# Two generated filters in a two-block kernel: where the first transform weights are split, and where the second filter's modulations stand

## The reference

```python
mod = c_act @ mod_w[i] + mod_b[i]                       # 1024 x 6144, six vectors
u = causal_dwconv(u, dw_w) + dw_b                       # 31 taps, first block
# second block, filters of the Hyena branch
hdn = jnp.sin(freq * (hdn @ fw2 + fb2))
h = (hdn @ fw3 + fb3).reshape(L, HYENA_ORDER, 2, D_HYENA)
h = h * jnp.exp(-t * deltas)[:, None, None, :]
circ = jnp.concatenate([h_fwd, zeros, h_bwd[:0:-1]], axis=0)
return jnp.fft.rfft(circ, axis=0)                       # one for each of the two orders
```

## Time and profile before

| what | value |
|---|---|
| median of 3 runs | 3285.05 us (3284.10 to 3286.02) |
| profiled execution, its own time | 3293.38 us |
| its span | 3291.6 us |
| TensorE matmul busy | 3100.8 us, 94% |
| VectorE busy | 1710.9 us, 52% |
| ScalarE busy | 1012.1 us, 31% |
| GpSimd busy | 399.9 us, 12% |
| TensorE clock granted, mean | 0.962 |

### The profile page before, as it was taken

The page is one execution under the profiler, slowest core; times in us unless marked ns, Lnnn a source line. Parts: engine busy times, 40 slices in busy tenths (PEclk is TensorE's granted clock), DMA queues, the critical chain, the costliest instruction groups (busy, mean ns, idle before and its releaser), DMA issues. The chain is left out here.

```text
span 3291.6 us, 33493 instructions
## 1 busy us (share of the span) xinstructions
PE 3100.8 (94%) x13786; PEld 2500.3 (76%) x13786; DVE 1710.9 (52%) x1776; ACT 1012.1 (31%) x1203; POOL 399.9 (12%) x161
## 2 busy tenths in 40 slices
PE   7999869899999999899999999799999999999996
PEld 3784457778888888778888877677877788888885
DVE  5698886655655554574411176677455322223225
ACT  3455444332212222233221133476222311111111
POOL 0496540000000000000200144000110000000000
PEclk8998879899999999899999999899998999999998
DMA  5114423232222321322332343521331202112112
GB/s 207 58 33 160 161 82 115 76 104 71 96 83 97 122 86 63 108 77 77 124 113 103 117 151 124 133 62 50 128 114 58 76 26 64 48 39 61 39 45 109
DMA packets 96192, 301.24 MB, mean 92 GB/s; under 512 B 11205, under 2 KB 15045, under 8 KB 95847
## 3 DMA queue, kind: packets, MB, share of 16 engines
q1 hardware_dynamic: 96040, 299.09, 27.8%
HBM read 251.34 MB, written 47.71 MB: 91 GB/s over the span
## 5 line engine op out<-in xcount | busy, mean ns | idle before, releaser
L708 PE MATMUL ps<-mainr,wh 128*128 128x512 f32 (+1 forms) x6592 | 1781.8, 390 | 31.0 <-issue 12.7
L708 PEld LDWEIGHTS ps<-mainr,wh 128*128 128x128 f32 x6592 | 1238.4, 189 | 290.4 <-issue 34.5
L708 PE MATMUL ps<-mainr,wl 128*128 128x512 f32 (+1 forms) x3296 | 1029.8, 389 | 0.0
L708 PEld LDWEIGHTS ps<-mainr,wl 128*128 128x128 f32 x3296 | 622.6, 189 | 128.4
L1714 DVE TENSOR_TENSOR wl<-raw,wh 128x1024 fp32r<-128x1024 f32 (+2 forms) x272 | 294.6, 1085 | 459.4 <-ACT wh L1236 459.2
L1236 ACT CAST wh<-raw 128x1024 fp32r<-128x1024 f32 (+2 forms) x320 | 282.0, 885 | 750.3 <-PE ps L708 539.6
L1973 DVE TENSOR_TENSOR mainf<-mainf,ps 128x1024 f32<-128x1024 f32 x80 | 97.6, 1220 | 215.1 <-PE ps L708 215.1
L754 PE MATMUL ps<-mainr,wh 128*128 128x512 f32 x576 | 165.7, 412 | 36.4 <-issue 22.0
L2014 DVE SCALAR_TENSOR_TENSOR ps<-mainf,vec,ps 128x1024 f32<-128x1024 f32 (+1 forms) x174 | 181.0, 1103 | 2.5 <-ACT ps L1425 2.3
L2498 POOL TENSOR_TENSOR tmp<-tmp,mainf 128x1024 f32<-128x1024 f32 x8 | 27.5, 3439 | 1162.2 <-DMA mainf<-in_rope 1099.0
L2465 POOL TENSOR_TENSOR wl<-raw,wh 128x1024 fp32r<-128x1024 f32 x48 | 114.7, 2400 | 425.0 <-ACT wh L1236 425.0
(11 more groups left out here) (236 smaller groups left out, 2903.9 us busy)
## 6 DMA issues: line engine op xcount, KB each, us to landing
raw<-in_mod_w SPq DMA_DIRECT2D x48, 512.0 KB, 4.2
raw<-in_ada_w SPq DMA_DIRECT2D x48, 512.0 KB, 3.6
raw<-in_f_up SPq DMA_DIRECT2D x44, 512.0 KB, 4.0
raw<-in_g_up SPq DMA_DIRECT2D x44, 512.0 KB, 3.5
raw<-in_w_in SPq DMA_DIRECT2D x40, 512.0 KB, 4.1
raw<-in_pw SPq DMA_DIRECT2D x24, 512.0 KB, 3.8
sc_x<-mainf SPq DMA_DIRECT2D x24, 512.0 KB, 2.6
mainf<-sc_x SPq DMA_DIRECT2D x24, 512.0 KB, 6.7
```

The source lines that it names most:

```text
L708: ins = e.matmul(out, wt[:, a:b], xs[n], start=kk == 0 and t == 0, stop=kk == kt - 1 and t == 2)
```

## The change

Two things. First, the two functions `modulation_weights` on ScalarE and VectorE are taken out, with their calls. The first two weight tiles of each filter's transform are split at the end of step 7 of the filter instead, behind the lower halves of its taps and the convolution step after them on VectorE, and behind the upper halves on ScalarE. Second, in the second filter the modulations stand behind steps 0, 4 and 6, where they stood behind 0, 3 and 5. In the first they stay behind 0, 3 and 5. What is computed is the same, and so are the list of weights and the number of instructions.

```diff
     for s in range(32):
         out.append(("f", s))
-        if s % 16 in (0, 3, 5):
+        if s in (0, 3, 5, 16, 20, 22):
             out.append(next(mods))
...
-    def modulation_weights(kind, jb, ahead):
-        for kp in range(4):
-            split_to(k.W[kind, jb, kp] + ahead)
...   scalar_program, filter_step, behind the upper halves
                 e.copy(k.TAPS_OF(0, step)[:, n, :], k.BANK("taps", o, step, n)).then_inc(*k.to("thi", o, step, n))
+            if step == 7:
+                split_to(k.W["filt", o, 0, 0] + 2)
             return
...   scalar_program and vector_program, walk through OTHER
         else:
-            modulation_weights(kind, s, HL)
             row = (kind, s)
...   vector_program, filter_step, behind the lower halves
             conv_steps(turns, 1)
+            if step == 7:
+                split_to(k.W["filt", o, 0, 0] + 2)
             return
```

## The result

The changed kernel takes 3292.29 us in the median of 19 runs (3287.27 to 3296.84); the kernel before takes 3282.99 in 19 runs beside them (3280.68 to 3287.34). The ratio is 1.0027, with a 95% interval of 1.0021 to 1.0033: **9.3 us slower**, between 6.9 and 10.8 by the interval. Forecast were 3293.7 us and +8.6. Spans and times of single executions of one kernel differ by several us, so a stage is compared by its own rows.

A forecast was written before the change was run, and what follows sets the result against it. Tap steps are bound by a loop through three engines, product steps by TensorE (first filter) and VectorE (second). Terms 3.0 + 5.3 + 0.3 = +8.6 us on 3285.05 gave 3293.7 us, range 3288.5 to 3298.5.

The forecast's parts named there:

- The wait that goes: Behind the third modulation: lower halves of the taps come 3.61 us earlier in the first filter, 2.44 in the second.
- The late first product: First filter, step 8: TensorE waits for VectorE's lower halves, convolution and split, starting 3.94 us later than before.
- Its speed: Step 8's product in each filter, partly at half-speed clock after a standstill: 7.6 us taken, 5.39 at full clock.
- No cover: Behind the first products: TensorE full in the first filter, VectorE in the second, so the whole delay passes on.
- The middle modulation: Second filter: one more sparse step before it may start it at the lower clock; 0 to 0.66 us, +0.3 taken.
- Loads keep up: Second filter: raw tiles of the moved modulations are asked for one modulation ahead, so no term for loads.
- The sum: First filter +3.0, second filter +5.3, middle modulation +0.3: +8.6 us in all.
- The anchor: Median of the kernel before, taken as 3285.05 us, on which the forecast of 3293.7 us stands.
- GpSimd first: Rival: GpSimd takes the shared port before VectorE's split, +2.2 us in each filter, +13.0 in all; chance 0.15.
- The clock that stays up: Rival: both first products take 5.39 us, 2.2 less each, +4.2 in all, 3289.3 us; chance 0.12.
- The shift of the port's phase: Rival, second filter's tail: VectorE's splits and sums meet no GpSimd, saving 13.4 us, -4.8 in all; chance 0.08.
- The hidden start: Rival: waits gained count in full and the late first product is hidden by slack, -6.0 us, 3279.0; chance 0.05.

The follow-up runs named there:

- splits-alone kernel: Changed kernel with the second filter's modulations back behind steps 0, 3 and 5, so only the weight splits moved; 3293.15 us against 3284.49, ratio 1.0024.
- the kernel that kept TensorE busy: Changed kernel plus 28 and 22 extra, overwritten matmuls ahead of the first product in the two filters; 3289.19 us, ratio 1.0013 of before.

## Why the prediction was right, and where its sizes were off

- **The wait that goes.** Expected 3.61 us. In the changed kernel the lower halves of step 6 come 11.30 us behind the third modulation's start (279.95 to 291.25), where they came 14.91 behind it (280.36, to 295.27): 3.61. In the second filter 2.44 was expected. The splits-alone kernel, whose modulations stand as before, shows it in its second profile: step 7's lower halves came 16.07 us behind the third modulation's start (383.90 to 399.97), where before they came 18.52 behind it (380.01, to 398.53), 2.45 less. The size of this wait hangs on when the loads land: in the second profile of before the two casts waited 2.58 and 1.03 us for them, where they waited 2.35 and 0.28 in the first, and the lower halves came 20.03 us behind.
- **The late first product.** Expected 3.94 us later; 19.79 for 15.85 us is 3.94, and 19.79 for 15.81 in the second profiles is 3.98. The three parts (lower halves, convolution, split) stood as computed, and VectorE came first at the port by 0.21 us where 0.23 was computed.
- **Its speed.** I took 7.6 us for each of the two first products, between bounds of 7.05 and 8.15. Measured were 8.11 and 7.28 in the first profile, 7.51 and 7.18 in the second: the mean was about right, and that the clock is the cause is shown by the kernel that kept TensorE busy. The 5.39 us at full clock was 0.25 short: from a product's start to its copy a step takes 5.64, since a step's first matmul starts before the copy of the one before it.
- **No cover.** Steps 9 to 15 took 37.9 us in both profiles of both kernels, and the tail 66.3 to 66.8: TensorE in the first filter and VectorE in the second pass on everything. Right.
- **The filters one by one.** They were less exact than the sum. To the first filter's copy 3.0 us were forecast, and 3.5 measured in the first pair of profiles (27.90 and 24.40), 4.4 in the second (27.31 and 22.91): step 8 before took 8.55 us in the execution from which I computed, and 7.10 in the other. For the second filter 5.6 were forecast (5.3 and 0.3), and 6.3 and 4.9 measured.
- **The middle modulation.** Mis-sized in both pairs: +0.3 us taken, 0.66 the bound, +0.89 (9.99 for 9.10) and +0.64 (9.80 for 9.16) measured. The upper bound was the first filter's 9.76 us, and this one ran even a little slower. No term stood for the second filter's first modulation, with its wait for a load inside it: it took 11.27 and 9.84 us before and 11.69 and 11.42 in the changed kernel. "Loads keep up" holds for the moved modulations, not for this one, which waited 2.6 to 3.0 us for its last tile in both kernels.
- **The sum.** 8.6 us forecast; 10.0 in the first pair of profiles (197.9 and 187.9), 9.0 in the second (196.5 and 187.6), 9.3 in the times.
- **What stood on luck.** The parts of the sum that came out exactly are chains of waits. Where the clock falls differs between executions, and single terms were off by up to 1.6 us for that, in both directions. The anchor was not exact either: with more runs the kernel before is at 3282.99 us and not 3285.05, and the forecast time was 1.4 us too high for that although the step was 0.7 too small.
- **The rivals.** GpSimd first did not happen. Made to happen, it cost what the rows say for a lead of 0.72 us: 2.39 + 1.08 - 0.72 - 1.23 = 1.52 us, measured 1.48. The clock that stays up did not happen by itself; made to happen it gave 3.2 to 3.9 of the 4.4 us. The shift of the port's phase did not happen: in the tail the long weight splits took 3.17, 3.35 and 2.30 us (3.15, 3.36 and 2.30 before), and the four sums 3.2 to 3.4 as before. The hidden start did not happen.

## What to carry to other kernels

A split of weights that stalls two engines may still be in the right place if the engine behind them needs its result early: before moving it, compute the start of the first instruction that reads it, by the chain ahead of its new place, and put it at the earliest point at which its data are there and no wait stands. Here, in the first filter, the wait of 3.6 us was seen and removed, and 7.1 to 8.0 were paid one step later; with both splits directly behind step 6, the wait is gone and the first product starts 2.0 us earlier than before. Where TensorE works at the low clock behind a standstill, look for the same in the kernel before: here both kernels had it, and it was no part of the loss. Where a trace differs between executions, count from an event behind the last variable one, and take a second profile before a difference of 2 us in one stage is explained.

## What the runs showed of the hardware

- With GpSimd's addition started 0.72 us ahead, VectorE's subtraction of two SBUF tiles lost 1.48 us, and with VectorE 0.21 us ahead GpSimd's addition showed 3.22 us for 2.35. In both, the one that started first kept its own duration, and the one that started second ended later by the time that the other still needed; the wait shows as a longer instruction, not as idle time. The Trainium skill, SBUF — State Buffer, in its section on SBUF's two separate sides, says of the port pair that the two engines share that the one that starts first has it for the whole instruction and the other blocks, and these runs agree.
- TensorE's granted clock fell during the standstills of 8.6 and 5.5 us (means of 0.70 and 0.68), and the next 5.2 and 3.3 us of dense matmuls ran at 0.50 to 0.51 of the clock, the 1.2 GHz level. In the kernel before it was still 1.00 over a standstill of 2.7 us (288.43 to 291.12) and 0.55 over the few matmuls of the 5.1 us behind it. 28 matmuls ahead (6.68 us) kept it at 1.00 over a gap of 1.10 us.
- A modulation of 16 records took 7.03 us at a granted clock of 1.00, 8.7 at 0.80, 9.3 at 0.75 and 10.0 at 0.70. The first one of the kernel before took 7.03 in one execution and 9.32 in another.
